# A two-block transformer kernel: biases ahead of the turns, a tile chain in halves, a rope step moved, and a shared closing

## The reference, cut to what matters

```
# block 1
h = modulate(rmsnorm(x));  q,k,v,u = split(h @ w_in)
x = x + g1 * (concat(diff_attention(q,k,v), s5(u)) @ w_out)
h = modulate(rmsnorm(x));  top 4 of 32 experts for each token
y = sum over the token's experts of gate * (((clip(up)+1) * swish(gate_in)) @ w2[e] + b2[e])
x = rmsnorm(x + g2 * y) * final_g
# block 2
h = modulate(rmsnorm(x) * g_norm)
x_rnn, z_rnn, q, k, v, z_attn, g_r, g_a = split(h @ w_in_2)     # each 1024 wide
for each of 8 heads:
    xc = conv4(x_rnn);  hr = rg_lru(xc)                          # a linear scan over tokens
    q, k = partial_rope(q), partial_rope(k)                      # the first 32 of 128 rows are rotated
    o = attention(q, k, v) * silu(z_attn);   r = hr * silu(z_rnn)
merged = sigmoid(g_r) * (r @ w_out_rnn) + sigmoid(g_a) * (o @ w_out_attn)
x = x + gate * (merged @ w_o)
out = rmsnorm(x) * g_final
```

## Time and profile before

| what | value |
|---|---|
| median of 3 runs | 2006.65 us (2000.22, 2009.47, 2006.65) |
| time of the profiled execution | 2001.55 us |
| its span | 2000.2 us |
| PE (TensorE) busy | 1934.6 us, 97% |
| DVE (VectorE) busy | 850.0 us, 42% |
| ACT (ScalarE) busy | 420.7 us, 21% |
| POOL (GpSimd) busy | 237.2 us, 12% |
| mean granted TensorE clock | 0.991 |
| mean DMA rate | 280 GB/s read and written over the span |

### The profile page before, as it was taken

How to read it: one execution, slowest core, us unless ns; L and a number is a source line. 1 busy time by engine, 2 the same in 40 slices (tenths; PEclk the granted TensorE clock), 3 DMA queues, 4 the chain that set the end, 5 groups by cost and what they waited for, 6 DMA issues and landing times.

```text
span 2000.2 us, 38353 instructions
## 1 busy us (share of the span) xinstructions
PE 1934.6 (97%) x16479; PEld 1080.3 (54%) x16479; DVE 850.0 (42%) x1548; ACT 420.7 (21%) x905; POOL 237.2 (12%) x171
## 2 busy tenths in 40 slices
PE   8999999999999999999999999989999999999998
PEld 4455544333434343444333343445687877888887
DVE  5989875111121111112111111115567677764465
ACT  3223513111111010101111010102234433431101
POOL 0000000000000000000000000011443434360011
PEclk9999999999999999999999999999999999999999
DMA  8475797998899999999999999964121212122221
GB/s 338 132 280 198 286 349 310 419 420 361 320 421 419 420 420 421 420 420 420 420 418 420 418 418 418 419 268 195 65 89 66 69 66 88 66 85 85 85 85 63
DMA packets 103419, 553.94 MB, mean 277 GB/s; under 512 B 14224, under 2 KB 25488, under 8 KB 48336
## 3 DMA queue, kind: packets, MB, share of 16 engines
q1 hardware_dynamic: 81472, 517.23, 64.1%
q10 hardware_dynamic: 14720, 17.43, 2.6%
q0 software_dynamic: 7056, 16.79, 2.3%
HBM read 532.91 MB, written 26.35 MB: 280 GB/s over the span
## 4 chain that ended last, share of the span: by engine, by line
PE 68%; DMA 14%; SPq 9%; DVE 6%; issue 2%; ACT 1%; POOL 0%; ACTq 0%; DVEq 0%; POOLq 0%
PE psum L1106 21%; PE psum L923 19%; PE psum L931 9%; DMA arena<-in_w 9%; SPq L467 8%; PE psum L594 6%; PE psum L1066 3%; DMA ring<-in_w 2%; DMA arena<-in_mod_slabs 1%; PE psum L916 1%; PE psum L1184 1%; PE psum L903 1%; PE psum L778 1%; PE psum L939 1%; DMA h_rows<-ring 1%
## 5 line engine op out<-in xcount | busy, mean ns | idle before, releaser
L923 PE MATMUL psum<-arena,ring 128*32 128x512 f32 x4096 | 450.7, 593 | 13.1 <-DMA arena<-in_w 12.6
L923 PEld LDWEIGHTS psum<-arena,ring 128*32 128x32 f32 x4096 | 134.1, 110 | 309.9 <-issue 307.6
L2096 DVE TENSOR_SCALAR h_t<-psum 128x512 f32<-128x512 f32 (+2 forms) x33 | 27.9, 845 | 571.4 <-PE psum L923 571.4
L931 PE MATMUL psum<-arena,h_t 128*32 128x256 f32 x3840 | 217.8, 380 | 3.9 <-DMA arena<-in_w 3.0
L1450 ACT ACTIVATE ring<-psum,mods,gain 128x64 f32<-128x64 f32 (+2 forms) x264 | 85.6, 429 | 607.1 <-PE psum L903 607.1
L931 PEld LDWEIGHTS psum<-arena,h_t 128*32 128x32 f32 x3840 | 121.1, 110 | 100.2 <-issue 18.7
L1106 PE MATMUL psum<-ring 128*128 128x256 f32 x768 | 171.1, 380 | 0.0
L2415 POOL DMA_INDIRECT ring<-h_rows,row_i x33 | 35.6, 1078 | 1138.4 <-PE psum L903 830.5
L1106 PEld LDWEIGHTS psum<-ring 128*128 128x128 f32 x768 | 146.2, 190 | 19.8 <-issue 0.3
L1106 PE MATMUL psum<-h_t,ring 128*128 128x256 f32 x672 | 154.4, 380 | 0.3 <-ACT arena L1522 0.3
L923 PE MATMUL psum<-ring 128*32 128x512 f32 x1344 | 148.8, 593 | 5.9 <-DMA ring<-in_w 5.8
(11 more groups left out here) (477 smaller groups left out, 2138.3 us busy)
## 6 DMA issues: line engine op xcount, KB each, us to landing
arena<-in_w SPq DMA_DIRECT2D x288, 1024.0 KB, 27.8
ring<-in_w SPq DMA_DIRECT2D x96, 1024.0 KB, 29.2
ring<-in_pairs SPq DMA_DIRECT2D x40, 1024.0 KB, 4.8
ring<-in_dot_slabs SPq DMA_DIRECT2D x40, 512.0 KB, 5.7
ring<-in_mod_slabs SPq DMA_DIRECT2D x6, 2048.0 KB, 11.6
ring<-in_proj_slabs SPq DMA_DIRECT2D x24, 512.0 KB, 4.4
y_rows<-arena SPq DMA_DIRECT2D x3, 3584.0 KB, 25.0
y_rows<-work ACTq DMA_DIRECT2D x72, 64.0 KB, 7.6
```

The costliest lines, as they stand in the source:

```text
L923: mm = pe.matmul(psum[32 * j:32 * j + 32, g, :], x_e[:, c * tokens + g * TG:c * tokens + g * TG + TG], slot[s][:, j * S:(j + 1) * S], star ...
L931: mm = pe.matmul(psum[32 * j:32 * j + 32, 6 + g // 2, (g % 2) * 256:(g % 2) * 256 + 256], h_e[:, g * 256 + half * P + 32 * c:g * 256 + hal ...
L2096: dve.tensor_scalar(gate, psum[:, 0:groups, 0:256], LIMIT, None, ALU.min).then_inc(sem("gate clipped"), 1)
```

## The change

Four edits.

1. **Last store.** Of the four DMAs that store the last pass, ScalarE issues two and SP the two others, behind SP's first load of v weights.
2. **Tile chain.** TensorE writes the biases of tiles 0, 1 and 2 ahead of the first turn; nine `keep_on` products become six, and two new ones stand between `norm_sums(0)` and `spread_scale(0)`. `turn_sum`, `residual`, `tile_squares` and `norm_sums` hand the tile over in two halves of four k each, with one semaphore step for each half, and the squares are two ScalarE operations instead of one.
3. **Odd heads.** In heads 1, 3 and 5 the rotation of k moves from ahead of the recurrence to behind `block_22`; in odd heads `block_22` moves ahead of the gating of z. In all heads `u2_of` moves two recurrence operations forward.
4. **Closing.** TensorE adds the squares held in k = 0 ahead of the seventh product of the last pair, and those of k = 6, tokens 0 to 255, straight behind it. ScalarE loads the table of the root early, by a root over four columns that nobody reads any more (`std1`). Output rows 0 and 1 are multiplied by `g_final` on ScalarE behind pair 2 of the last four; the spread scale is written to a second bank, ScalarE copies it to SBUF, GpSimd multiplies the two rows by it, and ScalarE issues their DMAs. VectorE and SP keep rows 2 to 7.

```diff
@@ -473,6 +473,9 @@
             load_v(0)
+            sp.wait_ge(sem("y kept"), NP)
+            for j in range(2, 4):
+                store_quarter(sp, NP - 1, j)
@@ -524,8 +527,8 @@
-            for k in range(KT):
-                sp.wait_ge(sem("out made"), k + 1)
+            for k in range(2, KT):
+                sp.wait_ge(sem("out made"), k - 1)
                 sp.dma_start(io["out"][:, k * S:(k + 1) * S], x_t[:, k, :]).then_inc(sem("out stored"), 16)
@@ -1028,7 +1031,7 @@
                 if t == 3:
-                    pe.wait_ge(sem("moe added"), 2)
+                    pe.wait_ge(sem("moe added"), 4)
                 for k in range(KT):
@@ -1040,11 +1043,13 @@
                     mm = pe.matmul(psum[:, a + k // 4, (k % 4) * P:(k % 4 + 1) * P], parts[:, t * TOPK, k * P:(k + 1) * P], identity, start=False, stop=True, skip_group_check=True)
-                mm.then_inc(sem("sum turned"), 1)
+                    if k % 4 == 3:
+                        mm.then_inc(sem("sum turned"), 1)
             def norm_sums(t):
-                pe.wait_ge(sem("tile squares"), t + 1)
                 for k in range(KT):
+                    if k % 4 == 0:
+                        pe.wait_ge(sem("tile squares"), 2 * t + k // 4 + 1)
                     mm = pe.matmul(psum[:, 1, 2 * t:2 * t + 2], h_t[:, k, t * P:(t + 1) * P], norm_parts[:, k, :], start=(k == 0), stop=(k == KT - 1), skip_group_check=True)
@@ -1070,13 +1075,14 @@
             second_bias(0)
-            keep_on(9, 0)
+            second_bias(1)
+            second_bias(2)
+            keep_on(6, 0)
             turn_sum(0)
-            second_bias(1)
             keep_on(2, 0)
             norm_sums(0)
+            keep_on(2, 0)
             spread_scale(0)
-            second_bias(2)
             turn_sum(1)
@@ -1105,6 +1111,11 @@
                 mm.then_inc(sem("products"), 1)
+
+            def token_squares(k, tiles, first=False, last=False):
+                for t in tiles:
+                    mm = pe.matmul(psum[:, 1, t:t + 1], h_t[:, k, t * P:(t + 1) * P], ones[:, 0:1], start=(first and t == 0), stop=last, skip_group_check=True)
+                return mm
@@ -1163,6 +1174,10 @@
                     pe.wait_ge(sem("last merged sums"), 3)
+                if n == len(PAIRS) - 1:
+                    pe.wait_ge(sem("squares added"), 6 + 5)
+                    token_squares(0, range(TT), first=True)
+                    pe.wait_ge(sem("norm squares"), 16 + 4 * 3 + 2)
                 product(block_q, second[:, 4:8, :], t4)
@@ -1209,24 +1224,17 @@
                 pair_ended(n)
-
-
-            def token_squares(k, tiles, first=False, last=False):
-                for t in tiles:
-                    mm = pe.matmul(psum[:, 1, t:t + 1], h_t[:, k, t * P:(t + 1) * P], ones[:, 0:1], start=(first and t == 0), stop=last, skip_group_check=True)
-                return mm
-
-            pe.wait_ge(sem("squares added"), 6 + 5)
-            token_squares(0, range(TT), first=True)
+            token_squares(6, (0, 1))
             pe.wait_ge(sem("norm squares"), 16 + 4 * 4 - 1)
-            token_squares(6, range(TT))
+            token_squares(6, (2, 3))
             token_squares(7, (2, 3), last=True)
...
             pe.wait_ge(sem("tile scale"), TT + 2)
-            for t in range(TT):
-                mm = pe.matmul(psum[:, 0, t * P:(t + 1) * P], last_scale[:, t:t + 1].to_broadcast([P, P]), identity, start=True, stop=True, is_transpose=True, skip_group_check=True)
-            mm.then_inc(sem("scale spread"), 1)
+            for bank in range(2):
+                for t in range(TT):
+                    mm = pe.matmul(psum[:, bank, t * P:(t + 1) * P], last_scale[:, t:t + 1].to_broadcast([P, P]), identity, start=True, stop=True, is_transpose=True, skip_group_check=True)
+                mm.then_inc(sem("scale spread"), 1)
@@ -1457,14 +1465,14 @@
-            def store_y(q):
+            def store_y(q, quarters=range(4)):
                 groups = PASSES[q][2]
...
                 act.wait_ge(sem("y kept"), q + 1)
-                for j in range(4):
+                for j in quarters:
                     store_quarter(act, q, j)
@@ -1482,7 +1490,7 @@
                     store_y(q - 1)
-            store_y(NP - 1)
+            store_y(NP - 1, range(2))
@@ -1505,8 +1513,10 @@
             def tile_squares(t):
-                act.wait_ge(sem("moe added"), t + 1)
-                act.activation(h_t[:, :, t * P:(t + 1) * P], x_t[:, :, t * P:(t + 1) * P], ACT.Square).then_inc(sem("tile squares"), 1)
+                for half in range(2):
+                    ks = slice(4 * half, 4 * half + 4)
+                    act.wait_ge(sem("moe added"), 2 * t + half + 1)
+                    act.activation(h_t[:, ks, t * P:(t + 1) * P], x_t[:, ks, t * P:(t + 1) * P], ACT.Square).then_inc(sem("tile squares"), 1)
@@ -1643,8 +1653,19 @@
                         act.activation(h_t[:, k, part], x_t[:, k, part], ACT.Square).then_inc(sem("norm squares"), 1)
+                        if j == 3 and m == 1:
+                            act.activation(std1, std1, ACT.Sqrt)
+                    if j == 2:
+                        for k in range(2):
+                            act.activation(x_t[:, k, :], x_t[:, k, :], ACT.Copy, scale=col("g_final", k)).then_inc(sem("last rows scaled"), 1)
             act.wait_ge(sem("norm sum"), 3)
             act.activation(last_std, psum[:, 1, 0:TT], ACT.Sqrt, bias=const("eps"), scale=1.0 / D).then_inc(sem("norm root"), 1)
+            act.wait_ge(sem("scale spread"), TT + 3)
+            act.wait_ge(sem("x mixed"), 8 + 16)
+            act.activation(y_pair[:, 0, :], psum[:, 1, :], ACT.Copy).then_inc(sem("last rows scaled"), 1)
+            for k in range(2):
+                act.wait_ge(sem("row made"), k + 1)
+                act.dma_start(io["out"][:, k * S:(k + 1) * S], x_t[:, k, :]).then_inc(sem("out stored"), 16)
@@ -2156,11 +2177,13 @@
             def residual(t):
-                dve.wait_ge(sem("sum turned"), t + 1)
                 for k in range(KT):
+                    if k % 4 == 0:
+                        dve.wait_ge(sem("sum turned"), 2 * t + k // 4 + 1)
                     x_part = x_t[:, k, t * P:(t + 1) * P]
                     ins = dve.scalar_tensor_tensor(x_part, psum[:, SUM_AT[t] + k // 4, (k % 4) * P:(k % 4 + 1) * P], g2[:, k:k + 1], x_part, ALU.mult, ALU.add)
-                ins.then_inc(sem("moe added"), 1)
+                    if k % 4 == 3:
+                        ins.then_inc(sem("moe added"), 1)
@@ -2168,7 +2191,7 @@
                 dve.wait_ge(sem("scale spread"), t + 1)
-                dve.wait_ge(sem("moe added"), t + 1)
+                dve.wait_ge(sem("moe added"), 2 * t + 2)
                 for k in range(KT):
@@ -2211,7 +2234,7 @@
             dve.wait_ge(sem("scale spread"), TT + 1)
-            dve.wait_ge(sem("moe added"), TT)
+            dve.wait_ge(sem("moe added"), 2 * TT)
             for k in range(KT):
@@ -2316,24 +2339,28 @@
                     rope(i + 1, 0)
-                    rope(i + 1, 1)
                 dve.wait_ge(sem("a made"), 2 * i + 2)
...
                 then(dve.tensor_tensor(tanh_g, tanh_g, at_zero, ALU.max))
+                u2_of(next_pair + 1)
                 then(dve.tensor_tensor(i_g, i_g, xc, ALU.mult))
                 then(dve.tensor_tensor(i_g, i_g, tanh_g, ALU.mult))
-                u2_of(next_pair + 1)
                 dve.tensor_tensor_scan(b_g, a_g, i_g, 0.0, ALU.mult, ALU.add).then_inc(sem("decayed"), 1)
...
                 u4_of(next_pair + 1)
+                if i % 2:
+                    block_22(next_pair + 1, rows_of(next_pair + 1)[1][:, back])
+                    if i + 1 < HEADS2:
+                        rope(i + 1, 1)
                 dve.wait_ge(sem("z sig"), 2 * i + 2)
...
                 dve.tensor_tensor(za, za, z_sig, ALU.mult).then_inc(sem("z gated"), 1)
-                block_22(next_pair + 1, rows_of(next_pair + 1)[1][:, back])
+                if i % 2 == 0:
+                    block_22(next_pair + 1, rows_of(next_pair + 1)[1][:, back])
                 dve.wait_ge(sem("z gated"), 2 * i + 2)
@@ -2500,6 +2527,9 @@
                 pool.tensor_tensor(h_t[:, 0, :], h_t[:, 0, :], h_t[:, k, :], ALU.add).then_inc(sem("squares added"), 1)
+            pool.wait_ge(sem("last rows scaled"), 3)
+            for k in range(2):
+                pool.tensor_tensor(x_t[:, k, :], x_t[:, k, :], y_pair[:, 0, :], ALU.mult).then_inc(sem("row made"), 1)
```

## The result

The changed kernel takes 1996.84 us (median of 6 runs, 1993.05 to 2000.81), the kernel before 2009.8 us (6 runs, 2000.22 to 2013.7) on the same chip: ratio 0.9941, interval 0.9917 to 0.9965. Timed again later beside its variants it gave 0.9941 once more, interval 0.9927 to 0.9956. By the ratio that is 11.9 us of 2009, while the two medians differ by 13.0; the prediction's sum was 13.0 and its forecast 1992, range 1985 to 2001.

The account below looks back on a forecast made before the run. The prediction took weight loads to bound the expert stage, untouched by the change, with TensorE holding 68% of the chain. Heads 9.6, tile chain 3.6 and closing -0.2 sum to 13.0 us; off 2005.4 that forecasts 1992, range 1985 to 2001.

Parts of the forecast that it names:

- the new wait: Heads: gate products would wait 0.3 us for the masks, three times, 0.9 in all.
- stall and slow product: Heads 3 and 5: removing the 2.04 us stall also restores the product behind it, from 2.94 and 3.08 to 1.73.
- Rival (a): Odd heads: the stall moves instead of going; heads give 5 us, sum 8.4, time 1997; chance 0.16.
- Rival (c): Heads: GpSimd's sums catch the moved rotation, `block_22` over 1 us late; 3.4 us slower, 2009; chance 0.04.
- moving `u2_of` changes the order, not the sum; its product was made long before: Heads: moving `u2_of` forward was claimed to add no time, its input being ready long before.
- The store's term: Tile chain: two queues issue the last store 1.0 to 2.0 us earlier; gain 1.2, bounds 0 and 2.3.
- the 1.4 put down to it: Last store: sharing saves only issuing time, at most 1.4 of its 2.79 us.
- it can't: the second half of its weights landed at 1375.0: Tile chain: `v_rows(0, 1)` must wait for weights until 1375.0 instead of starting at 1373.4, leaving a 2.4 us gain.
- still at turn 0's release: Tile chain: biases and six products take 10.5 us instead of 9.7, still ending when turn 0 is released.
- The prediction's clock step: Tile chain: TensorE idles 1.6 to 2.2 us ahead of the spread, so its clock may fall; turn 1 takes 1.7 longer.
- Rival (b): Tile chain: clock falls and v weights come no earlier; chain gives 1.0 us, sum 10.4, time 1995; chance 0.12.
- The early table buys nothing: Closing: the root starts at 1991.55 instead of 1991.38 despite its early table load, 0.15 us later.

Follow-up runs that it names:

- Experiment six: Changed kernel with head 7's `u2_of`, the first squares and all output rows put back as before: 1992.31 us against 2008.98 before, ratio 0.9923.
- experiment eight: Changed kernel with four filling products ahead of the three biases, one behind, and closing and head 7 put back: 1988.91 us against 2000.99 before, ratio 0.9938.
- best1: Same kernel as experiment eight, four filling products ahead of the biases and closing put back on the changed kernel: 1988.91 us, ratio 0.9938 to before.
- experiment two: Kernel before with only the shared last store and the tile chain's edit: 2006.12 us against 2008.98, ratio 0.9984.

## Why the prediction was right, and where not

**Heads: right, in mechanism and size.** Forecast 9.4 for heads 1, 3, 5 and 0.2 for head 7; the pair of profiles shows 9.28 up to head 7's scores, the timing of the edit alone 9.4, with an interval of 6.2 to 12.5. The six steps from the scores of head 1 to those of head 7 came out as -2.30, +0.31, -3.25, -0.43, -3.36 and -0.25 us. By the prediction's terms they are -2.3, +0.3 (the new wait), -3.25 (stall and slow product), -0.43 (slow scores of 0.73 gone, new wait), -3.39 and -0.29. Only how the new 0.3 divides was not foreseen: the gate products wait 0.12 (1.84 for 1.72), and the scores take the other 0.19 (2.31 to 2.35 for 2.16), since the head's gate is late for them. The sum is the forecast one because the masks come when reckoned, and time lost in the scores is not lost again there. Rival (a) falls. Rival (c) needed `block_22` over 1 us later than reckoned. It was forecast to end at 1533.5 and ended at 1535.69 in a profile whose head 1 lies 1.96 later, so 0.2 late, and the rotation ran at 0.67 to 0.68 per operation, with no GpSimd beside it.

**Missed: what head 7 does.** The step "moving `u2_of` changes the order, not the sum; its product was made long before" failed. In head 7 its input, ScalarE's copy of the product, is 0.70 late, and TensorE then waits 0.85 two pairs on, where VectorE's reserve is small because three slab sums take 2.7 to 2.8 each. Experiment six takes half a microsecond of it back.

**Tile chain: the size was right in the median (3.2 for 3.6), by errors that cancel.**
The store's term was mis-sized: 1.2 taken, 2.18 to 2.27 measured in every profile with it, near the bound of 2.3. Nearly all of it is issuing: the store that lands last is issued 1.04 behind the copy of y in experiment eight (1336.68) and 2.95 before (1336.98), 1.9 sooner, and its landing takes 3.47 instead of 3.76. The prediction's own bound for this was "1.0 to 2.0 earlier"; it took the low end. The Trainium skill (DMA: Bandwidth & Descriptors, "Issuing engines are not separate DMA queues") allows only the issuing time. The trace agrees to 0.3 us; the 1.4 put down to it was too small.
The step "it can't: the second half of its weights landed at 1375.0" was wrong, and it was a misreading. The row groups two loads, 14.6 and 23.6 us, and I gave the longer one to the second. In the trace of before, the load issued at 1351.39 is the one of 14.6 and landed at 1366.0. No profile shows a wait of `v_rows(0, 1)` for `ring<-in_v_slabs`. Without that bound the sum for the chain would have been 3.9 + 1.2 = 5.1 (with the store as measured, 6.1), and best1 shows 4.9.
The timing shows 3.2, 1.7 less than best1. That is what both profiles of the timed kernel lose behind head 1's stall (experiment two), a term the prediction didn't have. Inside the chain two more things scatter the result, and no run shows what they take on average, since the order of before has them too (112.2 in one profile).
The first is the low stretch ahead of turn 0. The biases and filling products were priced at 10.5 us, "still at turn 0's release"; they took 10.9 from 1338.72 in experiment six and 15.2 from 1343.36 in the kernel after. The prediction's clock step looked only at the idle ahead of the spread. There it was right to expect another fall: in nine of the eleven profiles with the new chain or a variant of it the clock was low again around the spread, and turn 1 took 2.7 to 3.8 instead of 2.05 in seven of them (1.7 longer was reckoned).
The second is the late starts, which no term held.
Rival (b), with 1.0 for the chain, was right for the first profile. The timing speaks against it (3.2), but its 1.0 lies inside the interval.

**Closing: right in mechanism, a little more lost.** Forecast 0.2 lost, and 0.4 was. The squares cost 0.95 (0.91 forecast), and the stores set the end (7.68 for 7.60). The root started 2.12 behind the last product instead of 2.73, so it was 0.33 late (0.17 forecast). "The early table buys nothing" holds only against the kernel before: the last square ends at 1984.11, and a table load of 1.28 behind it would have put the root near 1985.4 (an estimate) instead of 1984.81. Heads alone and the full change take nearly the same from the pairs to the end, 555.05 and 554.97, but in the former's profile the rows started 0.46 later behind the root than in the kernel before, with the clock low in the spread.

**The base.** The sum was taken off the mean of three runs, 2005.4; the later median was 2009.8. That is why 1992 was 4.8 us below the median measured, though the gain (11.9 for 13.0) was within 1.1.

## What to carry to other kernels

A row that shows minimum, median and maximum of two transfers doesn't say which is which: ask for the window of the one that a bound rests on. Filling products that keep an engine at its clock are instructions ahead of the real work; when the clock is low they take longer (48 of them 7.17 us for 4.03 here), and they then delay what they were meant to speed up. Before one profile is read as the effect of an edit, look at the same stretch in a second profile of the same kernel, and time the parts of a change apart.
